# Moving four waits and one block of VectorE work around the scan stage of a fused two-block transformer kernel

## The reference

```python
def mixer_hgrn2(u, mem_kv, w_in, lb_fwd, lb_bwd, norm_g, w_out):
    q, i, zf, zb, gate, xq = split(u @ w_in)      # 8 heads of 128 columns each
    q = silu(q)
    f = lb + (1 - lb) * sigmoid(z)                # for zf and zb; k = 1 - f
    o = gla_chunked(q, k_f, v, log f_f) + flip(gla_chunked(flip q, flip k_b, flip v, flip log f_b))
    o = rmsnorm(o, norm_g) * silu(gate)
    return concat([o, memory_cross_attn(xq, mem_kv)]) @ w_out

def second_block(...):                            # per layer
    h = h + rmsnorm(mixer(rmsnorm(h, g0)), g1)
    h = h + rmsnorm(conv_ffn_2(rmsnorm(h, g2)), g3)
```

## Time and profile before

| | us |
|---|---|
| median of 3 runs | 1487.23 (1483.44 to 1487.77) |
| the profiled execution | 1484.44 |
| its span in the profile | 1483.1 |
| PE busy | 1423.4 (96%) |
| DVE busy | 932.0 (63%) |
| ACT busy | 724.0 (49%) |
| POOL busy | 231.7 (16%) |

### The profile page before, as it was taken

One profiled execution on the slowest core, in us unless ns is written; L12 is line 12 of the kernel. 1 busy time (PEld: TensorE's weight loads), 2 busy tenths in 40 slices (PEclk: granted clock), 3 DMA queues, 4 the chain that ended last, 5 costly groups with the idle time before them and its releaser, 6 DMA issues.

```text
span 1483.1 us, 23163 instructions
## 1 busy us (share of the span) xinstructions
PE 1423.4 (96%) x9623; PEld 1264.5 (85%) x9623; DVE 932.0 (63%) x1506; ACT 724.0 (49%) x1054; POOL 231.7 (16%) x190
## 2 busy tenths in 40 slices
PE   6899999999999999998999999999999998799998
PEld 5887799999898899996776799999689987699997
DVE  5744476667784866676456165656465787665655
ACT  4434345555452445553655355444457775554453
POOL 2571200000000000002622500000133333100000
PEclk9999999999998999999999999999999999999999
DMA  8332145655463456452412355555344434355551
GB/s 302 140 129 114 58 171 176 236 181 190 174 231 128 163 179 227 173 197 96 160 58 86 114 199 185 213 192 178 137 172 146 143 118 157 137 187 180 205 198 57
DMA packets 36554, 240.40 MB, mean 162 GB/s; under 512 B 3873, under 2 KB 6241, under 8 KB 8930
## 3 DMA queue, kind: packets, MB, share of 16 engines
q1 hardware_dynamic: 36450, 238.92, 44.3%
HBM read 236.27 MB, written 2.64 MB: 161 GB/s over the span
## 4 chain that ended last, share of the span: by engine, by line
PE 87%; DVE 6%; ACT 2%; POOL 2%; issue 2%; DMA 0%; SPq 0%; ACTq 0%; DVEq 0%
PE ps L359 24%; PE ps L326 16%; PE ps L328 16%; PE ps L327 16%; PE ps L481 2%; PE ps L488 2%; POOL wlo L276 2%; PE ps L810 1%; PE ps L1615 1%; ACT whi L268 1%; PE ps L469 1%; DVE gb L2078 1%; PE ps L978 1%; DVE wlo L283 1%; PE ps L708 1%
## 5 line engine op out<-in xcount | busy, mean ns | idle before, releaser
L326 PE MATMUL ps<-XS,whi 128*128 128x256 f32 x2088 | 599.2, 287 | 17.8 <-POOL wlo L276 4.9
L327 PE MATMUL ps<-XS,whi 128*128 128x256 f32 x2088 | 594.8, 285 | 0.0
L328 PE MATMUL ps<-XS,wlo 128*128 128x256 f32 x2088 | 594.6, 285 | 0.0
L283 DVE TENSOR_TENSOR wlo<-raw,whi 128x2048 fp32r<-128x2048 f32 x163 | 372.5, 2287 | 126.7 <-ACT whi L268 126.4
L268 ACT ACTIVATE whi<-raw 128x2048 fp32r<-128x2048 f32 x204 | 388.8, 1907 | 117.8 <-PE ps L359 79.3
L326 PEld LDWEIGHTS ps<-XS,whi 128*128 128x128 f32 x2088 | 405.0, 194 | 24.1 <-issue 12.8
L327 PEld LDWEIGHTS ps<-XS,whi 128*128 128x128 f32 x2088 | 404.9, 194 | 1.8 <-issue 0.2
L328 PEld LDWEIGHTS ps<-XS,wlo 128*128 128x128 f32 x2088 | 404.6, 194 | 0.0
L359 PE MATMUL ps<-whi,MS 128*128 128x512 f32 x1024 | 292.5, 392 | 5.9 <-POOL wlo L276 3.5
L276 POOL TENSOR_TENSOR wlo<-raw,whi 128x512 fp32r<-128x512 f32 x162 | 214.8, 1362 | 502.3 <-ACT whi L268 429.4
L359 PEld LDWEIGHTS ps<-whi,MS 128*128 128x128 f32 x1024 | 189.3, 188 | 46.2 <-POOL wlo L276 4.3
(11 more groups left out here) (282 smaller groups left out, 1360.8 us busy)
## 6 DMA issues: line engine op xcount, KB each, us to landing
raw<-in_up SPq DMA_DIRECT2D x88, 1024.0 KB, 4.8
raw<-in_down SPq DMA_DIRECT2D x44, 1024.0 KB, 4.8
raw<-in_hg_t SPq DMA_DIRECT2D x16, 1024.0 KB, 4.8
raw<-in_od_t SPq DMA_DIRECT2D x8, 1024.0 KB, 4.9
raw<-in_ev_a SPq DMA_DIRECT2D x7, 1024.0 KB, 8.0
raw<-in_wa_o SPq DMA_DIRECT2D x6, 1024.0 KB, 4.8
raw<-in_hg_o SPq DMA_DIRECT2D x6, 1024.0 KB, 4.7
raw<-in_ev_o SPq DMA_DIRECT2D x4, 1024.0 KB, 7.0
```

Of the source, the lines that this page charges most:

```text
L283: ve.tensor_tensor(lo[:, 0:w], r[:, 0:w], hi[:, 0:w].bitcast(F32), ALU.subtract).then_inc(w_lo_v)
L326: pe.matmul(d, hi[:, c], S[:, k, 0:256], start=(k == 0), stop=False)
L327: pe.matmul(d, hi[:, c], S[:, k, 256:512], start=False, stop=False)
L328: last = pe.matmul(d, lo[:, c], S[:, k, 0:256], start=False, stop=(k == 7))
```

## The change

It has five edits. accumulate waits for each of its tiles just before the first use instead of for all at the start. In norm 5 ScalarE's high part of the first hg_x tile comes before the second half's xs_act. In the scan loop VectorE does masked_dve(n - 2) before differences_dve(n - 1). GpSimd waits for the factors of head 7 (h_fa at 8) before the low parts behind its loop. SyncE loads all tiles of the stage before the two gains.

```diff
@@ accumulate
             times = SCHED[tiles[-1]][3]
-            got = [(i,) + weights(m) for i, m in enumerate(tiles)]
+            got = [(i,) + parts_of(m) for i, m in enumerate(tiles)]
+            seen = -1
             whole = list(range((n + 511) // 512))
...
                 for some, hs in parts:
                     for i, hi, lo in some:
+                        if i > seen:
+                            weights(tiles[i])
+                            seen = i
                         for j in range(per):
@@ norm_act
             if n < 7:
                 xs_act(n, 0)
+                if n == 5:
+                    act_weights(NEXT[n] + 1)
                 xs_act(n, 1)
                 fill_act(n)
                 act_weights(NEXT[n] + 1)
@@ hgrn_dve
             for n in range(1, 11):
                 if n - 1 < 8:
                     gates_dve(n - 1)
-                    differences_dve(n - 1)
                 if 0 <= n - 2 < 8:
                     masked_dve(n - 2)
+                if n - 1 < 8:
+                    differences_dve(n - 1)
                 dve_weights(min(at_z(n + 1), LAST[6]))
@@ hgrn_pool
                 pool_weights(at_q(n + 1))
+
+            po.wait_ge(h_fa.sem, 8)
             pool_weights(NEXT[6])
@@ hgrn_sp
-            sp_weights(LAST[6] - 2)
+            sp_weights(LAST[6])
             next_gain_sp(6)
             gains_sp(6)
```

## The result

The changed kernel takes 1463.82 us (median of 4 executions, 1459.69 to 1466.05) against 1485.34 for the kernel before: a ratio of 0.9852 with a 95% interval of 0.9829 to 0.9875, so 22 us faster, 18 to 25 by the interval. The profiled execution took 1466.05 us.

The account below looks back on a forecast made before the run. TensorE, nearly always busy, bounds the kernel, so time comes only from its gaps or clock; 4.0 + 3.2 + 4.5 + 0.8 + 1.9 = 14.4 us off the mean 1485.7 gives 1471.3 us, range 1464 to 1480.

Parts of the forecast that it names:

- I take the upper one: Scan loop: each moved mask addition takes 1.36 us, held up by GpSimd's instruction, rather than the lower bound 0.22.
- about 1.3 us: Sign the prediction would be right: mask additions (L2105) at about 1.3 us instead of 0.22.
- The loop's sum of 16.0: Scan stage: a loop closing through GpSimd makes a head's period 16.0 us with handovers, as long as before.
- The rule that the prediction cited: VectorE instructions with two SBUF inputs and GpSimd instructions reading SBUF shut each other out for a whole instruction.
- The two heads' gain: Scan stage, moved masks: only the first two heads gain, 1.4 and 0.2 us; 0.8 left at head 7's gates.
- Rival (a): Scan stage: mask additions are not held up, period 14.69 us, total 1465.7 us; chance 0.20.
- 1.74 + 1.74 + 0.28 + 0.28 = 4.0: Single tile waits: gaps before the last pairs of two mixers and two feed-forwards vanish, 4.0 us.
- the forecast 14.4: Whole kernel: summed gain of all terms, 4.0 + 3.2 + 4.5 + 0.8 + 1.9 = 14.4 us.
- a near thing: Norm 5: the second hg_x tile's low part, done at 1080.95, just fits before TensorE wants it at 1081.2.
- the 3.2: Norm 5: the early high part of the first hg_x tile gains 3.2 us; ends 1.0 and 3.2.
- 2.1 for 1.9: Scan stage's end: the 1.90 us gap before the last pair goes, gaining 1.9 us.
- one term for TensorE's clock: Head 7: without the gap before its scores the slow clock behind it goes, gaining 0.8 us.

Follow-up runs that it names:

- r4: Changed kernel with the small masked block kept in PSUM, so each mask addition has one input there; ratio 0.9826 to the kernel before.
- r5: Kernel before with only the single tile waits in accumulate; ratio 0.9918, 12.2 us.
- r8: Kernel before with only GpSimd's wait for the factors of head 7 and the tile loads ahead of the gains; ratio 0.9944, 8.3 us.
- r9: Changed kernel with the last two tile loads behind the gain again; ratio 0.9883 to the kernel before.
- r11 to r14: Kernel before, single tile waits only at: even mixer's last pair, 0.9984; all but even mixer, 0.9966; first feed-forward's last pair, 1.0002; pairs behind odd mixer, 0.9966.
- r3: Changed kernel with the masks put back behind the differences; ratio 0.9899 to the kernel before.
- r1: Changed kernel measured once more against the kernel before, no edit; ratio 0.987, 5 executions from 1460.24 to 1469.07 us.

## Why the prediction was wrong, point by point

- **The masks, right.** "I take the upper one": the additions end with GpSimd's tile. The sign given for them, "about 1.3 us", was too high: they take up to 1.27 us but 0.75 each in the head shown, since 2.70 of the tile's 5.04 us were left when they began. The loop's sum of 16.0 was measured at 15.84, the wait went to the sums of squares, and r4 showed the cause by taking it away. The rule that the prediction cited from the Trainium skill, page "SBUF — State Buffer", section "Who interferes with whom", holds here for instructions of 32 partitions too, with 1.27 us against 0.22. The two heads' gain came out at 2.4 us by the seventh head, not 0.8, as the period was 15.84, not 16.0, and the third head still gained. Rival (a), whose 1465.7 lies closest to the median, got there by luck: the additions are held up.
- **Edit 1, the term of the sum that was mis-sized.** "1.74 + 1.74 + 0.28 + 0.28 = 4.0" measured 2.01, 2.02, 0.53 and 0.56, and with two more pairs 5.65. The timeline counts idle time from the modelled end of the last matmul. That one lasts 0.39 us, but the next would have started 0.23 us after its start, so each gap in the earlier trace rows is read 0.16 too short, and the first matmul behind a gap is slower by 0.1. The two more pairs (0.25 and 0.28 us) had gaps that this hides entirely. Together that is 1.65 of the 2.4 us by which the rows' 16.8 exceed the forecast 14.4.
- **Edit 2, right but for its last step and for the clock.** The second tile was "a near thing" and did not fit: its load, just behind the first of the row at 1053.07, was issued at 1060.81 and its high part began at 1066.23, over 5 us later instead of 4.5. So 0.46 us of a gap stayed, 0.7 by the matmuls' starts, and the 3.2 became 2.7. What the slow clock behind the old gap costs, 1.5 us in six of nine traces, the forecast put at nothing, since its trace did not show it.

```profile
1053.07 8.07 SPq L254 DMA_DIRECT2D raw<-in_hg_x  x2
1061.18 12.45 SPq L254 DMA_DIRECT2D raw<-in_hg_v  x3
...
1066.23 1.91 ACT L268 ACTIVATE whi<-raw 128x2048 fp32r<-128x2048 f32 x1 [2.90 <-DMA raw<-in_hg_x]
```

- **Edit 4, right.** All factors of head 7 at their free durations, the longest L2125 427 ns (1518 before), scores(7) with 0.22 of a gap. The clock behind it gave 1.4, not 0.8.
- **Edit 5 and the last pair, right in size** (2.1 for 1.9), less so in who brings it: edit 1 alone gives the 2.1 (r5), edits 4 and 5 alone 1.3 (r8). Edit 5 matters once edit 4 has moved the scores forward, and there r9 shows 1.6 us for it.
- **The step that failed most: the clock between executions.** The sum had one term for TensorE's clock, 0.8 us at head 7, and the range, which took 1464 from rival (a), allowed 1.5 us for the spread of executions. Executions of one kernel lie 9 us apart; of the 5.8 us between the first two traces of the changed kernel the odd mixer has 3.0, norm 3 has 1.5 and the first 170 us 1.2, all at stretches where the granted clock differs. With the rows' 16.8 us the time would be 1468.5. Over its three sets of executions the changed kernel took 1459.69 to 1469.07 in 13 executions, with a median of 1465.68, some 19 under the kernel before and inside the range; that the first four had a median below it is chance on top of the sizes.
- **Open.** That leaves 2.3 us of the median beyond the rows, and 4.1 of the mean (1464.3 against 1485.2). The slow clock that edit 2 removes is 1.0 of it on average. For the rest the granted clock of every execution is a measure: its mean is 0.9806 over 92 executions of the kernel before and 0.9846 over the 13 of the changed one. Twice what is missing to 1, times the span, is the time at the lower level: 57.6 and 45.0 us, 12.6 less. A stretch at the lower level costs at most half its length, so this is worth up to 6.3 us, of which 1.4 at head 7 and 1.0 behind hg_x are counted. So the changed kernel does run less at the lower level in stretches that it does not touch, and that is enough for what is missing. Edit 1 alone shows it as well (0.9820 over 6, against 0.9803 for the kernel before on the same chip). Its parts do not (0.9798 to 0.9809 in r11 to r14), and r3 and r9, which have edit 1 whole, show no more than head 7 and hg_x account for. In the odd mixer two of the nine traces of kernels with edit 1 whole (r1, r5) have no fall of the clock, and none of the nine others. No run shows how the change would do it; that cause stays open.

## What to carry to other kernels

Ask of every instruction that is moved what it will now run beside: the masks left TensorE's path and came under GpSimd's tile, and four tiny additions gave most of the gain back until one of their operands went to PSUM. A gap on a pipelined engine is longer than the idle time in the timeline, here by 0.16 us, the matmul's length less its usual distance to the next; compare starts. Before a range is given for a change of 1%, look at how far apart executions of the same kernel lie, and at which stretches the granted clock differs. One trace of the kernel before can be an uncommon one: here it lacked a fall of the clock that six of nine traces have, and had the longer of two falls elsewhere.

## What the runs showed of the hardware

- VectorE additions of 32 partitions x 64 elements with both inputs in SBUF took up to 1270 ns beside GpSimd's subtractions (median 394 over the launch); with one input in PSUM, beside the same subtractions, at most 229 (median 217).
- Two 1 MB loads and a 512 KB load issued within 1.1 us landed their first tile after 7.4 us (r9), and in the kernel before after 6.7, against a median of 4.8 for the heads' loads.
- In the odd mixer TensorE issued 17 to 19 matmuls in a stretch of 4 us without a gap, where a full stretch has 36. Behind it the granted clock was 0.50 for two stretches of 4 us, for one and a part, for part of one or for none in different executions, worth up to 4.5 us.
- Behind a gap of 3.2 us before the first hg_x product the clock fell in six of nine traces, for 1.5 us; without the gap in none of nine.
